# Nine expert slots in place of seven, and two units of each small expert round multiplied unsplit

## The reference, cut to what matters

```python
def moe_ffn(x, router_w, w1, w3, w2):
    logits = (xt @ router_w).astype(F32)
    top_v, top_i = lax.top_k(logits, TOP_K)
    ...
    for e in range(N_EXPERTS):
        y = y + gates[:, e:e + 1] * swiglu(xt, w1[e], w3[e], w2[e])
```

## Time and profile before

| | |
|---|---|
| median of 3 runs | 2364.59 us (2361.65 to 2365.38) |
| profiled execution, its own time | 2356.97 us |
| its span, first to last instruction | 2355.2 us |
| mean granted TensorE clock | 0.996 |
| transfers by HBM over the span | 579.02 MB read |
| expert rounds 1 to 7 in the span | 559.88 to 1447.45 us |

### The profile page before, as it was taken

One profiled execution on the slowest core, in us unless ns is written; L12 is line 12 of the kernel. 1 busy time (PEld: TensorE's weight loads), 2 busy tenths in 40 slices (PEclk: granted clock), 3 DMA queues, 4 the chain that ended last, 5 costly groups with the idle time before them and its releaser, 6 DMA issues.

```text
span 2355.2 us, 29291 instructions
## 1 busy us (share of the span) xinstructions
PE 2300.1 (98%) x11179; PEld 1890.5 (80%) x11179; DVE 1812.8 (77%) x2343; ACT 1392.4 (59%) x1588; POOL 31.7 (1%) x44
## 2 busy tenths in 40 slices
PE   8999999999999999999999998999999999999998
PEld 7788887887778887788778776888888888888887
DVE  5964568898875558998999898899775669987655
ACT  4444534677855447877887785565544545654543
POOL 0000000000000000000000000000000000000000
PEclk9999999999999999999999999999999999999999
DMA  8376543799976579999999995654565665455663
GB/s 283 106 223 188 183 156 100 298 362 359 396 281 215 196 238 368 402 397 373 395 404 380 370 402 223 196 160 143 170 199 187 185 210 162 121 175 168 201 187 125
DMA packets 212557, 582.10 MB, mean 247 GB/s; under 512 B 17228, under 2 KB 26584, under 8 KB 212281
## 3 DMA queue, kind: packets, MB, share of 16 engines
q1 hardware_dynamic: 210108, 571.87, 69.9%
q0 software_dynamic: 1872, 6.82, 0.8%
q10 hardware_dynamic: 428, 1.45, 0.2%
HBM read 579.02 MB, written 1.07 MB: 246 GB/s over the span
## 4 chain that ended last, share of the span: by engine, by line
PE 80%; DVE 9%; DMA 5%; ACT 4%; issue 1%; ACTq 0%; POOL 0%; SPq 0%; POOLq 0%; DVEq 0%
PE tile L895 21%; PE tile L897 21%; PE tile L896 21%; PE aux L1018 4%; DMA units<-in_moe_w 3%; DVE units_parts L2499 3%; PE aux L1362 2%; PE tile L1476 2%; PE tile L1477 2%; ACT high L1887 1%; DVE nat_parts L2499 1%; DVE k_buf_parts L2499 1%; PE tile L1374 1%; PE tile L1376 1%; DVE q_buf_parts L2499 1%
## 5 line engine op out<-in xcount | busy, mean ns | idle before, releaser
L2499 DVE TENSOR_TENSOR units_parts<-units,high 128x1024 fp32r<-128x1024 f32 (+3 forms) x357 | 523.9, 1485 | 108.3 <-ACT high L1887 105.8
L1887 ACT ACTIVATE high<-units 128x1024 fp32r<-128x1024 f32 (+3 forms) x357 | 448.0, 1273 | 184.4 <-PE tile L897 59.5
L896 PE MATMUL tile<-units_parts,acts 128*128 128x512 f32 (+2 forms) x1392 | 533.1, 383 | 0.0
L895 PE MATMUL tile<-high,acts 128*128 128x512 f32 (+2 forms) x1012 | 401.2, 396 | 6.2 <-DVE units_parts L2499 3.6
L897 PE MATMUL tile<-high,acts 128*128 128x512 f32 (+2 forms) x1012 | 389.7, 385 | 0.0
L896 PEld LDWEIGHTS tile<-units_parts,acts 128*128 128x128 f32 x1392 | 262.9, 189 | 47.9 <-issue 1.0
L895 PEld LDWEIGHTS tile<-high,acts 128*128 128x128 f32 x1012 | 191.3, 189 | 44.4 <-DVE units_parts L2499 5.7
L897 PEld LDWEIGHTS tile<-high,acts 128*128 128x128 f32 x1012 | 191.0, 189 | 38.7
L896 PE MATMUL tile<-units_parts,zbuf_parts 128*128 128x512 f32 x456 | 177.4, 389 | 0.0
L897 PE MATMUL tile<-high,zbuf_parts 128*128 128x512 f32 x368 | 143.3, 389 | 0.0
L2499 DVE TENSOR_TENSOR units_parts<-units,gbuf_parts 128x2048 fp32r<-128x2048 f32 x48 | 109.9, 2290 | 17.0 <-ACT gbuf_parts L1887 16.8
(11 more groups left out here) (527 smaller groups left out, 4869.1 us busy)
## 6 DMA issues: line engine op xcount, KB each, us to landing
units<-in_moe_w SPq DMA_DIRECT2D x192, 1024.0 KB, 7.2
units<-in_w_in SPq DMA_DIRECT2D x134, 512.0 KB, 3.8
units<-in_w_ff SPq DMA_DIRECT2D x128, 512.0 KB, 3.7
q_buf<-in_moe_w SPq DMA_DIRECT2D x48, 1024.0 KB, 7.7
k_buf<-in_moe_w SPq DMA_DIRECT2D x48, 1024.0 KB, 8.1
nat<-in_moe_w SPq DMA_DIRECT2D x48, 1024.0 KB, 7.3
units<-in_ffn_w SPq DMA_DIRECT2D x48, 512.0 KB, 4.2
units<-in_w_out SPq DMA_DIRECT2D x32, 512.0 KB, 3.6
```

What stands on the lines that cost most here:

```text
L895: nc.tensor.matmul(bank, lhs[0], high, start=start, stop=False)
L896: nc.tensor.matmul(bank, lhs[0], low, start=False, stop=False)
L1887: nc.scalar.activation(high_slot(SG[0], n) if wide_ else high_slot(SG[0], n)[:, 0:cols], halves(weights) if wide_ else weights[:, 0:cols], ...
L2499: V.tensor_tensor(low, weights, high, ALU.subtract).then_inc(SG[0].low_ready, 1)
```

## The change

Two things change, and what they need.

1. Two more slots. `bias2` is stored to HBM before the second layer, lent to expert units throughout, and loaded again for the second block. The first two rows of `gain` are lent too, but not while round 2 needs them. Which slot a unit takes, and how many units must be done before its load, is now set by a table built when the program is made: `EXPERTS`, a `Ring`. It gives each unit the open slot whose last unit is oldest, and `free` = the larger of that unit plus one and the third number of the slot's span.
2. In a small round the units k = 10 and 11 of w2 (`kept_whole`) are not split. PE waits for their transfer alone and multiplies the plain product (64 columns stationary) with the slot's float32 weights: 4 matmuls to a unit in place of 8. Neither ACT nor DVE touches these units, and tile 5's product is not split.

```diff
-EXPERT_COLS, EXPERT_UNITS, EXPERT_HIGHS = 2048, 7, 4
+EXPERT_COLS, EXPERT_UNITS, EXPERT_HIGHS = 2048, 9, 4
+EXPERT_OWN = 7
...
+GAIN_LENT = [(0, LARGE * MOE_UNITS, 1),
+             ((LARGE + 1) * MOE_UNITS + TURN_AFTER + 2, (N_EXP - 2) * MOE_UNITS + MOE_UNITS // 2,
+              (LARGE + 1) * MOE_UNITS + TURN_AFTER + 2)]
+EXPERTS = Ring(ROUNDS * MOE_UNITS, (EXPERT_OWN + 1) * [[(0, ROUNDS * MOE_UNITS, 0)]] + [GAIN_LENT])
+GAIN_FREE = 1 + EXPERTS.last[EXPERT_OWN + 1]
...
+def kept_whole(r):
+    return [MOE_UNITS - 2 * WHOLE + i for i in range(WHOLE)] if few(r) else []
...
-                return max(n - EXPERT_UNITS + 1, shared_)
+                if m < EXPERT_OWN:
+                    return lent[m - 3] if m >= 3 else 0
+                return len(STREAM1) + EXPERTS.free[m]
...
+                    sp.wait_ge(S.unit_done, FF1_AT)
+                    sp.dma_start(bias_kept.ap(), bias2[:, :, :]).then_inc(bias2_stored, 16)
...
+                        if l == 0:
+                            sp.dma_start(bias2[:, :, :], bias_kept.ap()).then_inc(bias2_loaded, 16)
...
+                            if MOE_UNITS - BACK_UNITS + k in kept_whole(r):
+                                row = k - (BACK_UNITS - 2 * WHOLE)
+                                if row == 0:
+                                    evacuated(folded)
+                                weights, product = whole_unit(), few_buffers(False, MOE_TILES - 2)[1]
+                                for h in range(2):
+                                    at = slice(h * 512, (h + 1) * 512)
+                                    for c in range(EXPERT_ROWS):
+                                        mm = nc.tensor.matmul(tiles[2 + h][0:FEW, :],
+                                                              product[:, EXPERT_ROWS * row + c, :],
+                                                              weights[:, c, at], start=False, stop=False)
+                                mm.then_inc(S.unit_done, 1)
+                                continue
...
-                    pool.wait_ge(S.unit_done, len(STREAM1) + (LARGE + 2) * MOE_UNITS)
+                    pool.wait_ge(S.unit_done, len(STREAM1) + GAIN_FREE)
...
-                    low_few(last - 1)
...
+                dve.wait_ge(bias2_loaded, 16)
```

More of the change, by code:

```diff
@@ L260, in stationary, with bisect_left, lows_before @@
     return slice(first, first + P)
+def bisect_left(values, v):
+    return sum(u < v for u in values)
+WHOLE = TILE_UNITS
+def kept_whole(r):
+    return [MOE_UNITS - 2 * WHOLE + i for i in range(WHOLE)] if few(r) else []
+SPLIT = [r * MOE_UNITS + m for r in range(ROUNDS) for m in range(MOE_UNITS) if m not in kept_whole(r)]
+SPLITS_BEFORE = [bisect_left(SPLIT, m) for m in range(ROUNDS * MOE_UNITS)]
+def lows_before(r):
+    return sum(MOE_TILES - 1 if few(q) else MOE_TILES for q in range(r) if few(q) or q == LARGE)
 def gather_columns(lots_):
@@ L629, in expert_unit, with kept, splits_before @@
             return n - len(STREAM1) if sig_ is S else -1
+        def kept(sig_, n):
+            m = expert_unit(sig_, n)
+            return m >= 0 and m % MOE_UNITS in kept_whole(m // MOE_UNITS)
+        def splits_before(sig_, n):
+            m = expert_unit(sig_, n)
+            return len(STREAM1) + SPLITS_BEFORE[m] if m >= 0 else n
         def slot(sig_, n):
@@ L634, in slot @@
             if m >= 0:
[L635 to L636 removed]
+                k = EXPERTS.slot[m]
+                return expert_ring[k], expert_lows[k], expert_loaded[k], EXPERTS.loads[m]
             where, raw, low = (RAW1, ring1, lows1) if sig_ is S else (RAW2, ring, lows)
@@ L888, in unit, with whole_unit @@
                 n = C.unit.take()
-                pe.wait_ge(SG[0].low_ready, n + 1)
+                pe.wait_ge(SG[0].low_ready, splits_before(SG[0], n) + 1)
                 low = slot(SG[0], n)[1]
                 return high_slot(SG[0], n), halves(low) if expert_unit(SG[0], n) >= 0 else low
+            def whole_unit():
+                weights, _, loaded, loads = slot(SG[0], C.unit.take())
+                pe.wait_ge(loaded, 16 * loads)
+                return halves(weights)
             def products(bank, lhs, high, low, start, stop):
@@ L2141, in few_tokens @@
                         used(TILE_UNITS)
-                        for t in (last - 2, last - 1):
-                            high_few(t, folded[t])
+                        high_few(last - 2, folded[last - 2])
                         act.wait_ge(S.unit_done, C.unit.n)
```

50 lines of the change are left out of this document (31 added, 19 removed).

## The result

The changed kernel takes 2373.64 us at the median of 13 runs (2368.09 to 2376.46), the kernel before, on the same chip, 2363.33 us (13 runs, 2356.54 to 2365.96). The ratio is 1.0043, with a 95% interval of 1.0035 to 1.0052: some 10 us slower, where 8.7 were forecast.

What follows compares the result with a forecast made beforehand. Round 4 was taken as bound by PE, small rounds by transfers and splitting side by side. Round 3's +10.9 and -2.2 for rounds 1, 5 and 7 gave +8.7 on 2364.6: 2373 us; 8 in 10 for 2362 to 2382.

Steps and rivals of the forecast that it cites:

- my case: Whole kernel: the main forecast, +8.7 us to 2373 us, own range 2368 to 2380; chance 0.67.
- Unit 129: Round 3: its load waits for unit 128, issued 890.19, landed 895.3, PE at 899.6, 9.8 us later; round 3 +10.9 us.
- lands 34 units on: Round 3: unit 163 (k = 9) lands at 983.0, 2.58 us to a unit, and is on PE at 987.3.
- the upper bound of +14: Round 3: +14 us if two stations lose up to 2.7 us to each other; +8 was the lower figure.
- The slots: Small rounds: room for two more landed units takes off DVE's waits for transfers, 2.7 us in rounds 1 and 5, 1.2 in 7.
- the three terms named: Round 5: 2.8, 0.9 and 0.7 us of DVE's 7.2 us of waits, at gather and scatter, put down to ACT's own order.
- round 3 like round 5: Rival, table misread or unit 129's wait met early: small rounds alone count, -2.2 - 1.3 us, 2361 us; chance 0.04.
- The unsplit units: Small rounds from k = 10: 3.43 us each on PE in place of 1.84, costing 1.4 us in rounds 1 and 5, 1.6 in 7.
- the cover: Behind k = 11: DVE has two split units ready during PE's 6.9 us unsplit, then a wide round; its spared work goes unused.
- Copies and gain loads: Store and reload of `bias2`: 0, without cover 2.6 us each; POOL's three gain loads moved from round 4 to 6: 0.
- the rival of a clock that stays down: Round 3: PE's clock stays at 1.2 GHz, some 30 units lose 0.8 us each, +25 us, 2398 us; chance 0.04.
- the list of signs: Profile after: PE still 9 to 10 us, round 3 some 11 us longer, rounds 1 and 5 at most 1.5 us shorter.

Runs made afterwards that it cites:

- e1: Changed kernel with the second span of `gain` opened seven units later, at unit 136, so no load waits for the unit just ahead; 2353.26 us, ratio 0.9971.
- e3: Kernel before, seven slots, all units split, with one change: the load of unit 129 waits until unit 128 is done, not unit 122; ratio 1.0064.
- e6: Kernel before, except that the load of unit 129 waits until unit 127 is done, one unit earlier than in e3; ratio 1.0017.
- e8: Kernel before with eight slots: `bias2` lent, `gain` not, every unit split, no load late; ratio 0.9960.
- e4: Kernel before with its seven slots and only the two unsplit units of each small round added, no copies of `bias2`; ratio 1.0026.
- e9: As e1, but small rounds take w2's rows in another order, so the unsplit units come second and third of w2; ratio 1.0007 against the kernel before.
- e7: Kernel before with only the copies of `bias2` added (stored to HBM, loaded again), no slot lent, no unit unsplit; ratio 0.9995.
- e11: The same kernel as e2, run again beside e9 on one chip; 2352.41 us, ratio 0.9962 against the kernel before.
- e2: As e1 (nine slots, no late load), but with every unit split, none kept unsplit; 2347.0 us, ratio 0.9940 against the kernel before.
- e10: Kernel before, except that the load of unit 171, the fourth of wide round 4, waits until unit 170 is done; ratio 1.0049.

## Why the prediction was right

**Sign, size and place.** Forecast +8.7 us with a chance of 0.71 for slower, measured 10.2 by the ratio and 12.0 by the rounds without round 2. The forecast for round 3 was +10.9 and it was +14.6; for rounds 1, 5 and 7 together -2.2, measured -1.95. Rounds 4 and 6 gave the other -0.6. So the mechanism and the place were right, round 3 was 3.7 us too small, and that the medians hide more than half of this miss is luck. The chances were added loosely: 0.71 counts all of my case, and 0.18 says it holds a little of it again.

**Unit 129** was read rightly from the table: transfer out at 890.0 (890.2), landed at 895.1 by ACT's start (895.3), PE at 899.4 (899.6). e1, e3 and e6 show by intervention that this load makes the loss, that nothing else is needed for it, and that the stream that is behind is what counts. The prediction named idle DMA engines ahead of the load; that they would be idle for 30 us, and that this leaves the stream six units behind, it did not say.

**Where round 3 was mis-sized.** The term that was too small is the step "lands 34 units on: 895.3 + 34 x 2.58 = 983.0, is on PE at 987.3", with DVE said to be 4 us ahead of the transfers. PE started k = 9 at 990.61, 3.3 us later. Two things, read from the trace. First, the stream's step is a little over 2.6 us: unit 154 (k = 0) starts on ACT, straight after its landing, at 960.82, so (960.8 - 895.1) / 25 = 2.63. Some stretch of it runs slower, where the last four units of w1 and w3 move in shorter rows: 388 GB/s from 945 to 956, 409 before and behind it; and unit 137 lands 3.4 us behind unit 136. Unit 163 was issued at 968.49 and landed 15.4 us later, at 983.9, 0.9 us after the forecast. Second, and more, the stations: ACT turned to the gather at 978.07 and took up units again at 981.75, three of them in a row, unit 163 at 985.36. DVE waited 3.0 us for the first and then had three units to do, so from landing to PE it is 6.7 us and not 4.3. I had that as "two stations with little between them lose a little to each other, up to the 2.7 us of the earlier trace rows", named it as the upper bound of +14, which the +14.6 passed, and took 0 for it. A queue that is empty pays for every detour of the stations behind it. That second part is argued from rows; no run took the gather out.

**The slots** gave 2.8 in round 5 and 3.0 in round 1, where 2.7 was forecast (7.2 less the three terms named is 2.8), in round 3 3.9 where the late load is absent (forecast as 1.3 net, "round 3 like round 5"). The reason that I gave, room for two units, is half wrong: e8 has room for one more and gains nearly as much.

**The unsplit units** cost what the sum said, 1.35 to 1.6 us a round, beside nine slots. The 8.6 that the prediction has for round 7 before is 8.5 by its own rows, which changes nothing. The units behind them are ready in time, with seven slots too (e4), so that part of the cover holds; at another place nothing is given back (e9). That they would be worth their 4.4 us "only at the head of a small round" has no support: nearer to the head they cost more, and at the head itself no run put them.

**Copies and gain loads** at 0: right by e7 for the copies; no run shows the gain loads apart. The clock was at 0.50 when PE went on and for some 4 to 5 us behind, then came back, as forecast, at no visible cost in round 3; the rival of a clock that stays down is out. PE's waits show none for `bias2`.

**What was off in the list of signs:** round 1 became 1.65 us shorter, and 1.5 was named as the limit; DVE's waits in round 5 fell only from 7.2 to 6.6 us in the first 94 (e11: 5.2), which is close to "as long as now", a sign of being wrong.

**A better version.** e2 and e11, the same kernel run twice, beat both the kernel before and the changed one: nine slots, the span of `gain` opened seven units later, and every unit split, 0.994 and 0.996 of the kernel before. Eight slots do as well within what can be told, and are simpler.

## What to carry to other kernels

When a buffer comes free late and an in-order queue deals out buffers by age, the newly freed one is the oldest and goes to the very next load: look in the table for the load with the shortest distance to the unit it waits for, not at the mean. If the stretch behind it lives on transfers, its price is how far the stream is behind when it runs again: the units that would have landed by then, times the time of one transfer. If the stretch lives on PE, it is PE's stop plus the slow clock behind it. Work taken off an engine counts only if that engine is late at that place and the written order lets it run on; and the first additional buffer may give all there is.

## What the runs showed of the hardware

The span changes between executions without any change in the work: e2 and e11 are one kernel, and their profiles differ by 6.6 us. The places are those in which the granted clock of PE is at 0.50 in one execution and not, or for less time, in another. In e2 it is 0.57 from 11 to 19 us, 1.00 from 364 to 379, 0.52 from 424 to 438 and 0.57 from 684 to 688; the changed kernel has 0.54 from 364 to 379 and 1.00 from 424 to 438. A comparison of two profiled executions had 16.6 us where the change made 10 by many runs; a sum over the rounds without round 2 had 12.0.

After a stop of 9.6 to 9.8 us the granted clock is 0.50 for 4 to 5 us (e10 and the changed kernel); after the stop of 0.9 us in e6 the matmuls of unit 129 follow each other at 0.23 us, the full pace.

A float32 matmul of 512 columns takes 0.87 us with 64 stationary columns (four in 3.49 us), and 0.86 with 128 (four in 3.43): the width of the stationary side made next to no difference, as the prediction took without a row for it.
